# Expert weights of a two-layer encoder trunk: neighbouring contraction rows on one partition, 8 KB runs

## The chip, the cores and the metric

One core of a Trainium2 chip runs the whole program. The metric is the device time in microseconds (us). Weights stream from HBM through DMA engines into SBUF; TensorE (PE) multiplies, and leaves its products in PSUM, from where VectorE (DVE) and ScalarE (ACT) take them. SyncE (SP) issues nearly all weight transfers, GpSimd (POOL) helps with small work.

## The reference, cut to what matters

x is 256 tokens of 1024 features. Each of two layers has a mixer and then a mixture of experts (MoE), both behind an RMS norm that is modulated by a conditioning vector c, and everything is float32:

```
mod = silu(c) @ ada_w[layer] + ada_b[layer]          # six vectors of 1024
sh_m, sc_m, g_m, sh_f, sc_f, g_f = split(mod, 6)
h = rmsnorm(x, norm_mix_g[layer]) * (1 + sc_m) + sh_m
x = x + g_m * mixer(h)                               # layer 0 attention and RG-LRU, layer 1 S5 and GLU
h = rmsnorm(x, norm_ffn_g[layer]) * (1 + sc_f) + sh_f
# one group of 4 out of 4 groups, then 2 of its 4 experts for each token:
out = sum over experts e of gates[:, e] * ((silu(h @ w1[e]) * (h @ w3[e])) @ w2[e])
x = x + g_f * out
```

w1 and w3 of an expert are 1024 x 512, w2 is 512 x 1024: 2 MiB each, 96 such matrices in two layers, about 201 of the 285 MB that the program moves. A sum over the contraction index may be taken in any order, which is what the change uses.

## The kernel before, in words

**Stages.** Conditioning products and the mixer of layer 0, the MoE of layer 0, the S5 and GLU mixer of layer 1, the MoE of layer 1, the final norm. Engines are programmed apart and meet at semaphores; every order is written out by hand.

**The ring.** All big weights pass through `ring`, six slots of 16 KB per partition, one 2 MiB tile in each. SP walks through a fixed list (`ORDER`, 12 tiles for a group of 4 experts) and, for tile n, waits until the product on tile n-6 is done, then issues the transfer (`send_expert`, L355). `moe_src` (L322) takes the source from `w1_v`, `w3_v`, `w2_v` (L316 to L318).

**Layout.** In `(k p) f -> p k f` partition p of a w1 or w3 tile holds rows p, 128+p, 256+p and so on: eight separate rows of 512 floats, 2 KB each in HBM. For w2 they are four rows of 4 KB. Block k of the contraction is then features 128k to 128k+127.

**MoE of a layer** (`ffn(L)` on each engine). PE turns the normed x, computes router logits, and DVE makes one-hot `pick` matrices. Then a loop of four expert groups. In each, `gather_block` (L1687) multiplies 128 columns of `xhat` (the operand that is loaded) by `pick` (the one that streams), for 8 blocks k and 2 token halves, which gives the picked tokens with features on partitions; `hg_evac` (ACT L799 for even k, DVE L1267 for odd) scales and shifts each block by `modA[:, n, k]` and `mod[:, L, SH_F, k]` on the way out of PSUM. `product_up` (L1657) multiplies w1 and w3 tiles, `turn_he` (L1670) transposes the gated hidden rows in blocks of 128 columns (`tr`, L1402, whose loaded operand is the data), `product_down` (L1675) multiplies by w2, `scatter` (L1702) adds back to tokens. A group whose experts all have at most 64 tokens runs in a narrow form of half the streamed columns: seven of the eight groups here; the first group of layer 1 runs wide.

**Modulation columns.** Conditioning products land as rows; `ada_cols(i)` (L1437) turns batch i of them into columns by 4 matmuls with `sel`, DVE's `mod_evac(i)` (L961) adds the bias columns, `mod_scale` (L973) forms (1+scale) times the norm's gain. Biases and gains come by small transfers on ACT's queue at the start (L610 to L626), and PE turns them (L1476 to L1478).

Of the kernel before, what the change touches and what calls it, by code (L numbers as in the profile page):

```python
# [16 lines left out]
ALU = mybir.AluOpType  # L17
# [52 lines left out]
SH_M, SC_M, G_M, SH_F, SC_F, G_F = range(6)  # L70

# [33 lines left out]
def build(nc, a, out):  # L105
    ctx = ExitStack()
    with ctx:
# [26 lines left out]
        condc = sb("condc", [P, KD])  # L134
        wr_f = sb("wr_f", [P, 2 * KD * NR + 12])
# [31 lines left out]
        brow = yg[0:6 * KD, 1, 0:2 * P].rearrange("r (l p) -> r l p", l=2)  # L167

# [65 lines left out]
        warm = rt[:, 319:320]  # L234
        by_bge = lambda ap: ap.rearrange("p (b g e) -> p b g e", b=NB, g=NG)
# [80 lines left out]
        w1_v = a["moe_w1"].rearrange("l e (k p) f -> l p e k f", p=P)  # L316
        w3_v = a["moe_w3"].rearrange("l e (k p) f -> l p e k f", p=P)
        w2_v = a["moe_w2"].rearrange("l e (k p) n -> l p e k n", p=P)  # L318
# [10 lines left out]
        def _(sp_):  # L329
# [23 lines left out]
            def send_expert(L, j, group):  # L353
                w, e = ORDER[j]
                sp_.dma_start(u3(MOE_BASE[L] + j, D if w == "w2" else FF), moe_src(L, w, group * EPG + e)).then_inc(  # L355
                    S(f"loaded{(MOE_BASE[L] + j) % SLOTS}"), 16)
# [34 lines left out]
            for L in range(2):  # L391
# [19 lines left out]
                with sp_.If(n_over > 0):  # L411
                    with sp_.Fori(0, EPG // 2) as ee:
                        for j in range(SLOTS):
                            w = ("w1", "w3", "w2")[j % 3]

                            sp_.wait_ge(S(f"over_used{L}"), ee * SLOTS + (j + 1))
                            cw = D if w == "w2" else FF
                            sp_.dma_start(u3(j, cw), moe_src(L, w, grp * EPG + ee * 2 + j // 3)).then_inc(
                                S(f"over_in{L}_{j}"), 16)

                    sp_.wait_ge(S(f"over_used{L}"), SLOTS + 3 * EPG)
# [182 lines left out]
        def _(act):  # L604
# [20 lines left out]
            for L in range(2):  # L625
                act.dma_start(brow[:, L, :], a["ada_b"][L].rearrange("(r p) -> r p", p=P)).then_inc(S("rows_in"), 16)  # L626
            act.wait_ge(S("c_ps"), 1)
# [23 lines left out]
            def modulate(n):  # L651

                L, sec = n // 2, (SH_M if n % 2 == 0 else SH_F)
                act.wait_ge(S("modA_ready"), n + 1)
                for k in (0, 1, 4, 5):
                    act.wait_ge(S("xT_ps"), 4 * n + k // 2 + 1)
                    s.activation(hT[:, k, :], bank[k // 2][:, (k % 2) * T:(k % 2 + 1) * T], ACT.Identity, scale=modA[:, n, k:k + 1],
                                 bias=mod[:, L, sec, k:k + 1]).then_inc(S("hT_act"), 1)

            def gate_row(n):  # L660
# [13 lines left out]
                S("cols_ready"), 1)  # L674

# [106 lines left out]
            def ffn(L):  # L782
# [11 lines left out]
                if L == 0:  # L794
                    table_evac(0, 4)

                def hg_evac(k, at):

                    return s.activation(hg[k], bank[at], ACT.Identity, scale=modA[:, n, k:k + 1],  # L799
                                        bias=mod[:, L, SH_F, k:k + 1])  # L800
# [108 lines left out]
        def _(dve):  # L909
# [51 lines left out]
            def mod_evac(i):  # L961

                lo, hi = BATCHES[i]
                dve.wait_ge(S("ada_cols_ps"), i + 1)
                src = bank[6 if i == 0 else 7][:, 0:4 * (hi - lo)]
                units = lambda ap: ap.rearrange("p (u c) -> p u c", c=4)
                v.tensor_tensor(units(mod[:, :, :, :].rearrange("p l s k -> p (l s k)")[:, 4 * lo:4 * hi]),
                                src.rearrange("p (c u) -> p u c", c=4),
                                units(adab[:, :, :].rearrange("p l n -> p (l n)")[:, 4 * lo:4 * hi]),
                                ALU.add).then_inc(S("mod_cols"), 1)  # L970
                dve.wait_ge(S("mod_cols"), i + 1)

            def mod_scale(n):  # L973
# [4 lines left out]
                dve.wait_ge(S("modA_ready"), n + 1)  # L978
# [175 lines left out]
            mod_scale(2)  # L1154

# [21 lines left out]
            def ffn(L):  # L1177
# [87 lines left out]
                def hg_evac(k, at):  # L1265

                    return v.tensor_scalar(hg[k], bank[at], modA[:, n, k:k + 1], mod[:, L, SH_F, k:k + 1], ALU.mult, ALU.add)  # L1267
# [117 lines left out]
            mod_scale(3)  # L1385

# [11 lines left out]
        def _(pe):  # L1398
# [38 lines left out]
            def ada_cols(i):  # L1437
# [249 lines left out]
            def gather_block(k, narrow, at):  # L1687

                n_s = 64 if narrow else P
                for b in range(NB):  # L1690
                    last = mm(bank[at].rearrange("p (e n) -> p e n", n=P)[:, :, 0:n_s], xhat[:, b, k * P:(k + 1) * P],  # L1691
# [344 lines left out]
```

## Time and profile before

| | |
|---|---|
| median of 3 runs | 905.07 us (904.87 to 907.25) |
| span of the profiled execution | 902.3 us |
| PE busy | 828.3 us, 92% |
| DVE, ACT, POOL busy | 329.6, 199.7, 147.0 us |
| moved by DMA | 285.33 MB, mean 316 GB/s |

The page gives the profiled execution's span, from its first to its last instruction, and no other time of its own; 2.8 us lie between it and the median of the runs. PE is a busy share of overlapping, pipelined records and says little about who waits in a given stretch. The page's row of GB/s, 40 slices of 22.6 us, shows two long plateaus: the two MoE stages.

### The profile page before, as it was taken

To read this page: it belongs to the slowest core of one execution; us is meant where nothing else is said; L and a number is where in the kernel's file an instruction comes from. 1 tells how busy PE (TensorE), PEld (TensorE's weight loads), DVE (VectorE), ACT (ScalarE), POOL (GpSimd) and SP (SyncE) were. 2 spreads that over 40 slices of the span, in tenths; PEclk is the share of its full clock that TensorE was granted. 3 is DMA by queue.
4 is the path that set the end of the run, shared out by engine and by line. 5 is a ranking of instruction groups with operands and counts; after the bars stand their busy time and mean duration, and the time that the engine had idled before them with its cause. 6 is when DMAs were issued, how large, how long until landed. Compare 5 with 4: busy or idle time off the path is not lost.

```text
span 902.3 us, 12803 instructions
## 1 busy us (share of the span) xinstructions
PE 828.3 (92%) x5243; PEld 452.2 (50%) x5244; DVE 329.6 (37%) x718; ACT 199.7 (22%) x329; POOL 147.0 (16%) x234
## 2 busy tenths in 40 slices
PE   3899989889999999999599999689999899999994
PEld 1377644554465564643456543434444554655641
DVE  1447994681141221410799410621000311312304
ACT  2402331521221311311500110411001212213112
POOL 2328678194000000000033100000000000000000
PEclk9999999999999999999899999889999999999997
DMA  9999999978999999997996882206867299999992
GB/s 327 330 379 383 359 392 264 380 265 331 389 397 398 390 394 397 392 392 276 400 381 227 315 324 94 94 1 224 317 236 252 98 392 395 392 398 392 395 399 91
DMA packets 126290, 285.33 MB, mean 316 GB/s; under 512 B 7093, under 2 KB 8389, under 8 KB 125993
## 3 DMA queue, kind: packets, MB, share of 16 engines
q1 hardware_dynamic: 123552, 277.88, 83.9%
q0 software_dynamic: 1984, 5.21, 1.9%
q10 hardware_dynamic: 712, 1.67, 0.5%
q8 instruction: 29, 0.48, 0.2%
q14 instruction: 13, 0.10, 0.0%
HBM read 279.50 MB, written 5.24 MB: 316 GB/s over the span
## 4 chain that ended last, share of the span: by engine, by line
PE 75%; DMA 10%; DVE 6%; SPq 6%; issue 1%; ACT 1%; DVEq 0%; ACTq 0%
PE PS L1664 17%; PE PS L1683 12%; PE PS L1691 8%; PE PS L1707 6%; PE PS L1970 6%; PE PS L1667 6%; DMA ring<-in_moe_w 4%; SPq L355 4%; DMA ring<-in_ada_w 4%; PE PS L1433 3%; PE PS L1505 3%; PE PS L1403 3%; DMA ring<-in_ab_w_in 2%; PE PS L1488 2%; SPq L364 2%; PE PS L1622 2%
## 5 line engine op out<-in xcount | busy, mean ns | idle before, releaser
L1683 PE MATMUL PS<-ring,work 128*64 128x512 f32 (+1 forms) x512 | 128.8, 595 | 0.5 <-DMA ring<-in_moe_w 0.5
L1664 PE MATMUL PS<-ring,hT 128*64 128x256 f32 x896 | 109.6, 387 | 4.9 <-DMA ring<-in_moe_w 4.9
L1664 PE MATMUL PS<-ring,yg 128*64 128x256 f32 x896 | 106.4, 379 | 0.0
L1278 DVE TENSOR_TENSOR work<-work,PS 128x512 f32<-128x512 f32 x32 | 22.0, 688 | 201.2 <-PE PS L1664 152.9
L1664 PEld LDWEIGHTS PS<-ring,hT 128*64 128x64 f32 x896 | 62.9, 139 | 47.9 <-issue 11.8
L1664 PEld LDWEIGHTS PS<-ring,yg 128*64 128x64 f32 x896 | 64.5, 137 | 32.7 <-issue 0.5
L1683 PEld LDWEIGHTS PS<-ring,work 128*64 128x64 f32 (+1 forms) x512 | 42.8, 143 | 75.4 <-issue 71.1
L1282 DVE COPY yg<-PS 128x512 f32<-128x512 f32 x32 | 22.1, 692 | 145.7 <-PE PS L1683 145.7
L1691 PE MATMUL PS<-work,xhat 128*128 128x256 f32 (+1 forms) x256 | 68.4, 427 | 7.5 <-issue 7.1
L1707 PE MATMUL PS<-yg,grow 64*128 64x512 f32 (+1 forms) x256 | 68.0, 606 | 0.0
L1691 PEld LDWEIGHTS PS<-work,xhat 128*128 128x128 f32 x256 | 50.1, 198 | 28.5 <-issue 21.9
L1970 PE MATMUL PS<-ring,yg 128*128 128x512 f32 x128 | 58.7, 603 | 0.0
L818 ACT ACTIVATE yg<-PS 128x512 f32<-128x512 f32 x32 | 19.1, 598 | 157.6 <-PE PS L1683 157.6
L598 POOL TENSOR_TENSOR work<-work 128x512 f32<-128x512 f32 x7 | 9.0, 1279 | 272.8 <-DVE work L1368 256.7
L1433 PE MATMUL PS<-ring,condz 128*32 128x512 f32 x320 | 40.4, 627 | 12.7 <-DMA ring<-in_ada_w 12.7
L809 ACT ACTIVATE work<-PS 128x512 f32<-128x512 f32 x32 | 19.1, 598 | 105.9 <-PE PS L1664 80.6
L1707 PEld LDWEIGHTS PS<-yg,grow 64*128 64x128 f32 (+1 forms) x256 | 25.8, 187 | 31.2 <-issue 31.2
L1970 PEld LDWEIGHTS PS<-ring,yg 128*128 128x128 f32 x128 | 23.2, 190 | 33.6 <-issue 33.6
L813 ACT ACTIVATE work<-PS 128x512 f32<-128x512 f32 x32 | 19.1, 596 | 80.7 <-PE PS L1403 80.7
L1403 PE MATMUL PS<-ident,work 128*128 128x128 f32 x176 | 29.7, 291 | 6.3 <-DVE work L1278 3.1
L1267 DVE TENSOR_SCALAR hT<-PS,modA,mod 128x512 f32<-128x512 f32 x16 | 13.0, 810 | 56.9 <-PE PS L1691 56.9
L1403 PEld LDWEIGHTS PS<-ident,work 128*128 128x128 f32 x176 | 19.7, 144 | 25.5 <-issue 21.5
(366 smaller groups left out, 995.5 us busy)
## 6 DMA issues: line engine op xcount, KB each, us to landing
ring<-in_moe_w SPq DMA_DIRECT2D x96, 2048.0 KB, 17.8
ring<-in_ada_w SPq DMA_DIRECT2D x20, 2048.0 KB, 15.5
work<-in_ada_w SPq DMA_DIRECT2D x4, 2048.0 KB, 14.6
ring<-in_s_glu_w SPq DMA_DIRECT2D x4, 2048.0 KB, 17.0
ring<-in_ab_w_in SPq DMA_DIRECT2D x3, 2048.0 KB, 25.3
ring<-in_ab_w_out SPq DMA_DIRECT2D x2, 2048.0 KB, 14.7
ring<-rot_tables SPq DMA_DIRECT2D x2, 2048.0 KB, 11.1
rot_tables<-grow POOLq DMA_DIRECT2D x8, 256.0 KB, 5.7
```

What stands on the lines that cost most here:

```text
L355: sp_.dma_start(u3(MOE_BASE[L] + j, D if w == "w2" else FF), moe_src(L, w, group * EPG + e)).then_inc(S(f"loaded{(MOE_BASE[L] + j) % SLOTS ...
L1278: v.tensor_tensor(he[:, e % 2, :], he[:, e % 2, :], bank[1], ALU.mult).then_inc(S("he_ready"), 1)
L1282: v.tensor_copy(yg[:, e % 2, HALF:], bank[1 if e == 3 else 3]).then_inc(S("y_dve"), 1)
L1403: return nc.tensor.transpose(dst, src, ident[0:n, 0:n])
L1433: last = mm(bank[7][32 * j:32 * j + 32, :], condz[:, k, 32 - r:64 - r], ada_unit(u)[:, k, :], start=any(first) and k < 4, stop=any(final) ...
L1505: last = mm(dst, w[:, k, :], hT[:, k, :], start=k == 0, stop=k == KD - 1)
L1664: last = mm(dst[64 * u:64 * u + 64, 0:256], hg[k][:, e * P:e * P + 64], w[:, k, 256 * u:256 * u + 256], start=k == 0, stop=k == KD - 1)
L1667: last = mm(dst, hg[k][:, e * P:(e + 1) * P], w[:, k, :], start=k == 0, stop=k == KD - 1)
L1683: last = mm(dst, left[:, at:at + (64 if narrow else P)], w[:, c4, h * HALF:(h + 1) * HALF], start=c4 == 0, stop=c4 == KF - 1)
L1691: last = mm(bank[at].rearrange("p (e n) -> p e n", n=P)[:, :, 0:n_s], xhat[:, b, k * P:(k + 1) * P], pick[:, b, :, 0:n_s], start=b == 0, s ...
L1707: last = mm(acc[2 * b + h], pickT[pp, e, b * P:(b + 1) * P], yg[pp, at, h * HALF:(h + 1) * HALF], start=False, stop=False)
L1970: last = mm(bank[GLU_BANK[m][part]], actT[:, k, b * P:(b + 1) * P], u3(n)[:, k, :], start=False, stop=k == KD - 1)
```

## The change

The expert matrices are cut so that neighbouring contraction rows share a partition. Of w1 and w3, partition p holds rows 4p to 4p+3 of each half of 512 rows: two runs of 8 KB. Of w2 it holds rows 2p and 2p+1 of each half of 256: also two runs of 8 KB. Block k of the contraction is now features 512*(k//4) + 4*m + k%4 for m of 0 to 127. What goes into the products follows: `gather_block` loads every fourth column of `xhat`, `turn_he` every second column of `he`, and the experts get their own modulation columns `mod4` in the new order, from four more small transfers at the start, four small transposes and three copies, four more matmuls in `ada_cols(1)` and in `ada_cols(2)` that load every fourth column of the conditioning rows, one more addition in `mod_evac(1)` and `mod_evac(2)` and one `mod_experts` for each layer. Products, slots, their order and all byte counts of the weights stay.

```
-        w1_v = a["moe_w1"].rearrange("l e (k p) f -> l p e k f", p=P)
-        w3_v = a["moe_w3"].rearrange("l e (k p) f -> l p e k f", p=P)
-        w2_v = a["moe_w2"].rearrange("l e (k p) n -> l p e k n", p=P)
+        w1_v = a["moe_w1"].rearrange("l e (h p c) f -> l p e h (c f)", h=2, c=4)
+        w3_v = a["moe_w3"].rearrange("l e (h p c) f -> l p e h (c f)", h=2, c=4)
+        w2_v = a["moe_w2"].rearrange("l e (u p c) n -> l p e u (c n)", u=2, c=2)
...
-                sp_.dma_start(u3(MOE_BASE[L] + j, D if w == "w2" else FF), moe_src(L, w, group * EPG + e)).then_inc(
+                sp_.dma_start(u3(MOE_BASE[L] + j, SLOT // 2), moe_src(L, w, group * EPG + e)).then_inc(
...
+                act.dma_start(row4[4 * L:4 * L + 4, :], a["ada_b"][L, SH_F * D:G_F * D].rearrange(
+                    "(r n) -> r n", n=HALF)).then_inc(S("rows_in"), 16)
+                act.dma_start(row4[8 + 2 * L:10 + 2 * L, :], a["norm_ffn_g"][L].rearrange("(r n) -> r n", n=HALF)).then_inc(
+                    S("rows_in"), 16)
...
+            row4_t = bank[5][:, P:P + 48].rearrange("p (c n) -> p c n", c=4)
+            s.activation(by_c(mod4[:, :, :, :].rearrange("p l s k -> p (l s k)")), row4_t[:, :, 0:8], ACT.Copy)
+            for L in range(2):
+                last = s.activation(by_c(gain4[L]), row4_t[:, :, 8 + 2 * L:10 + 2 * L], ACT.Copy)
...
+                if i:
+                    dve.wait_ge(S("cols_ready"), 2)
+                    m4 = by_c(mod4[:, i - 1, :, :].rearrange("p s k -> p (s k)"))
+                    v.tensor_tensor(m4, bank[7][:, P:P + 16].rearrange("p (c m) -> p c m", c=4), m4, ALU.add)
...
+            def mod_experts(L):
+
+                v.scalar_tensor_tensor(mod4[:, L, 1, :], mod4[:, L, 1, :], 1.0, gain4[L], ALU.add, ALU.mult).then_inc(
+                    S("modA_ready"), 1)
+                dve.wait_ge(S("modA_ready"), MODX_AT[L])
...
-                    return v.tensor_scalar(hg[k], bank[at], modA[:, n, k:k + 1], mod[:, L, SH_F, k:k + 1], ALU.mult, ALU.add)
+                    return v.tensor_scalar(hg[k], bank[at], mod4[:, L, 1, k:k + 1], mod4[:, L, 0, k:k + 1], ALU.mult, ALU.add)
...
+                if i:
+                    f = r + 2
+                    for c in range(4):
+                        last = mm(bank[7][:, P + 4 * c:P + 4 * c + 4], arows[i][:, c::4], sel[:, f:f + 4], start=True,
+                                  stop=True)
...
-            pe.wait_ge(S("rows_in"), 16 * (len(ROWS) + 2))
+            pe.wait_ge(S("rows_in"), 16 * (len(ROWS) + 6))
             tr(bank[4][:, 0:N_ROWS], rows, N_ROWS)
+            for c in range(4):
+                tr(bank[5][:, P + 12 * c:P + 12 * c + 12], row4[:, c::4], 12)
...
-                    last = tr(bank[dst][:, c4 * P:(c4 + 1) * P], src[:, c4 * P:(c4 + 1) * P])
+                    f = c4 // 2 * 2 * P
+                    last = tr(bank[dst][:, c4 * P:(c4 + 1) * P], src[:, f + c4 % 2:f + 2 * P:2])
...
-                    last = mm(bank[at].rearrange("p (e n) -> p e n", n=P)[:, :, 0:n_s], xhat[:, b, k * P:(k + 1) * P],
+                    last = mm(bank[at].rearrange("p (e n) -> p e n", n=P)[:, :, 0:n_s], xhat[:, b, f + k % 4:f + HALF:4],
```

On PE the list of instructions differs in three places by added rows. The one between the tiles of the layer-0 output projection (L1622, `mix_out`) stood before like this; L1443 is `ada_cols(1)`, L1468 `gate_row`:

```order
L1433 MATMUL PS<-ring,condz 32x512 x24
L1622 MATMUL PS<-ring,yg 128x512 x4
L1443 MATMUL PS<-sel,work 128x12 x4
L1622 MATMUL PS<-ring,yg 128x512 x4
L1468 MATMUL PS<-ident,mod 128x128 x8
L1622 MATMUL PS<-ring,yg 128x512 x8
```

and stands now like this (line numbers of the changed kernel):

```order
L1656 MATMUL PS<-ring,yg 128x512 x4
L1470 MATMUL PS<-sel,work 128x12 x4
L1475 MATMUL PS<-sel,work 128x4 x4
L1656 MATMUL PS<-ring,yg 128x512 x4
L1500 MATMUL PS<-ident,mod 128x128 x8
L1656 MATMUL PS<-ring,yg 128x512 x8
```

Four matmuls of 4 streamed columns are new; the same four stand in `ada_cols(2)` among the GLU products. On DVE the same moment, `mod_evac(1)` with its scalings before the first residual rows (L1174 `tmp`, L1160 `add_rows`), was

```order
L1151 TENSOR_TENSOR yg<-hT,work 128x1024
L967 TENSOR_TENSOR mod<-PS,adab 128x48
L976 SCALAR_TENSOR_TENSOR modA<-mod,cols 128x8 x2
L1174 TENSOR_TENSOR xhat<-PS,grow 128x512
L1160 TENSOR_TENSOR x<-x,xhat 128x512
```

and is now

```order
L1176 TENSOR_TENSOR yg<-hT,work 128x1024
L983 TENSOR_TENSOR mod<-PS,mod 128x4x4
L986 TENSOR_TENSOR mod<-PS,adab 128x48
L995 SCALAR_TENSOR_TENSOR modA<-mod,cols 128x8 x2
L1001 SCALAR_TENSOR_TENSOR mod<-mod,work 128x8
L1200 TENSOR_TENSOR xhat<-PS,grow 128x512
L1186 TENSOR_TENSOR x<-x,xhat 128x512
```

Two small operations are added and nothing changes its place.

## Rows read from the trace of the kernel before

**Rows 1.** The page: span, and GB/s in 40 slices.

```profile
span 902.3 us, 12803 instructions
...
GB/s 327 330 379 383 359 392 264 380 265 331 389 397 398 390 394 397 392 392 276 400 381 227 315 324 94 94 1 224 317 236 252 98 392 395 392 398 392 395 399 91
```

**Rows 2.** Windows, one expert group each: us, busy times (instructions), PEclk, DMA share, GB/s.

```profile
246.66:305.93 59.27, 59.26 (x403) 33.04 (x401) 13.59 (x31) 13.35 (x19) 0.00 (x0) 1.00 1.04 395
365.19:428.56 63.37, 60.14 (x403) 32.68 (x401) 13.60 (x31) 13.54 (x20) 0.00 (x0) 1.00 0.93 351
767.80:827.03 59.23, 59.22 (x402) 33.01 (x400) 13.59 (x31) 13.34 (x19) 0.00 (x0) 1.00 1.04 395
827.03:889.14 62.11, 59.92 (x402) 32.84 (x400) 13.59 (x31) 13.54 (x20) 0.00 (x0) 1.00 0.92 350
```

**Rows 3.** Chain of waits, last group of layer 0: start us, us, what.

```profile
365.26 7.10 PE PS L1691 x32
...
400.22 21.08 DMA ring<-in_moe_w
...
421.34 3.65 PE PS L1683 x16
```

**Rows 4.** Timeline of PE, same group: start, us, instructions, [idle before <-releaser].

```profile
405.76 1.95 PE L1664 MATMUL PS<-ring,hT 128*64 128x256 f32 x16 [1.00 <-DMA ring<-in_moe_w]
...
411.18 1.95 PE L1664 MATMUL PS<-ring,hT 128*64 128x256 f32 x16 [1.74 <-DMA ring<-in_moe_w]
```

**Rows 5.** Windows by DMA rate: long stream, 2 KB, mostly 4 KB, 16 KB packets.

```profile
211.00:420.00 209.00, 206.00 (x1392) 112.64 (x1390) 43.66 (x98) 44.21 (x64) 2.02 (x2) 1.00 1.04 391
257.50:262.50 5.00, 5.00 (x48) 3.30 (x44) 2.72 (x10) 1.06 (x2) 0.00 (x0) 1.00 1.05 386
279.50:288.50 9.00, 9.00 (x58) 4.04 (x56) 1.38 (x2) 1.20 (x2) 0.00 (x0) 1.00 1.03 405
430.00:436.00 6.00, 3.10 (x112) 2.54 (x102) 5.66 (x11) 5.54 (x13) 0.00 (x0) 1.00 1.01 421
```

**Rows 6.** Instructions of L1691 and L1933: duration ns min/median/max, first and last start.

```profile
L1691 PEld LDWEIGHTS PS<-work,xhat x256: 186/190/337, 178.3 to 833.6; 128*128 128x128 f32 x128
L1691 PE MATMUL PS<-work,xhat x256: 379/379/1190, 178.3 to 833.8; 128*128 128x256 f32 x112, 128*128 128x512 f32 x16
...
L1933 PE MATMUL PS<-hT,work x256: 268/270/578, 440.9 to 491.5; 32*128 32x128 f32 x128
```

**Rows 7.** Groups with their shapes: busy us, mean ns.

```profile
L1664 PEld LDWEIGHTS PS<-ring,yg 128*64 128x64 f32 x896 | 64.5, 137 | 32.7 <-issue 0.5
...
L1403 PE MATMUL PS<-ident,work 128*128 128x128 f32 x176 | 29.7, 291 | 6.3 <-DVE work L1278 3.1 <-DVE work L1257 2.8 <-ACT work L778 0.4
...
L1505 PEld LDWEIGHTS PS<-hT,ring 128*128 128x128 f32 x128 | 23.9, 190 | 4.9 <-issue 1.7
...
L1955 PE MATMUL PS<-work 128*32 128x128 f32 x128 | 6.5, 276 | 0.0
```

**Rows 8.** Chain of waits, 141 to 166 us: start us, us, what.

```profile
143.54 3.63 PE PS L1622 x8
147.18 0.79 PE PS L1443 x8
147.97 3.53 PE PS L1622 x8
```

**Rows 9.** Timeline of DVE, 148 to 155 us.

```profile
154.50 0.69 DVE L1174 TENSOR_TENSOR xhat<-PS,grow 128x512 f32<-128x512 f32 x1 [5.88 <-ACT grow L667]
```

**Rows 10.** Timeline of PE, 10 to 26 us.

```profile
13.15 3.64 PE L1433 MATMUL PS<-ring,condz 128*32 128x512 f32 x16 [8.73 <-DMA ring<-in_ada_w]
...
23.75 1.92 PE L1433 MATMUL PS<-ring,condz 128*32 128x512 f32 x16 [1.28 <-DMA ring<-in_ada_w]
```

**Rows 11.** Timeline of ACT and its queue, 5.8 to 9 us.

```profile
5.86 0.83 ACTq L626 DMA_DIRECT2D yg<-in_ada_b  x2
...
8.23 0.21 ACT L630 ACTIVATE condz<-condc 128x8 f32<-128x8 f32 x1
```

More of the change, by code:

```diff
@@ L70 @@
 SH_M, SC_M, G_M, SH_F, SC_F, G_F = range(6)
+MODA_AT = (1, 2, 3, 5)
+MODX_AT = (4, 6)
 PRIMED = dict.fromkeys(('he_ready', 'y_dve', 'heT_ready', 'y_act', 'sil_ready'), 1)
@@ L134, in build @@
         condc = sb("condc", [P, KD])
+        mod4 = sb("mod4", [P, 2, 2, KD])
         wr_f = sb("wr_f", [P, 2 * KD * NR + 12])
@@ L167, in build @@
         brow = yg[0:6 * KD, 1, 0:2 * P].rearrange("r (l p) -> r l p", l=2)
+        row4 = yg[0:12, 0, HALF:D]
         o = W0
@@ L234, in build @@
         warm = rt[:, 319:320]
+        gain4 = (w3(WORK - 8, KD), rt[:, 308:316])
+        by_c = lambda ap: ap.rearrange("p (m c) -> p c m", c=4)
         by_bge = lambda ap: ap.rearrange("p (b g e) -> p b g e", b=NB, g=NG)
@@ L416, in _ @@
                             sp_.wait_ge(S(f"over_used{L}"), ee * SLOTS + (j + 1))
-                            cw = D if w == "w2" else FF
-                            sp_.dma_start(u3(j, cw), moe_src(L, w, grp * EPG + ee * 2 + j // 3)).then_inc(
+                            sp_.dma_start(u3(j, SLOT // 2), moe_src(L, w, grp * EPG + ee * 2 + j // 3)).then_inc(
                                 S(f"over_in{L}_{j}"), 16)
@@ L653, in modulate @@
                 L, sec = n // 2, (SH_M if n % 2 == 0 else SH_F)
-                act.wait_ge(S("modA_ready"), n + 1)
+                act.wait_ge(S("modA_ready"), MODA_AT[n])
                 for k in (0, 1, 4, 5):
@@ L674, in _ @@
                 S("cols_ready"), 1)
+            row4_t = bank[5][:, P:P + 48].rearrange("p (c n) -> p c n", c=4)
+            s.activation(by_c(mod4[:, :, :, :].rearrange("p l s k -> p (l s k)")), row4_t[:, :, 0:8], ACT.Copy)
+            for L in range(2):
+                last = s.activation(by_c(gain4[L]), row4_t[:, :, 8 + 2 * L:10 + 2 * L], ACT.Copy)
+            last.then_inc(S("cols_ready"), 1)
             def rows_out(i):
@@ L795, in ffn @@
                     table_evac(0, 4)
+                act.wait_ge(S("modA_ready"), MODX_AT[L])
                 def hg_evac(k, at):
-                    return s.activation(hg[k], bank[at], ACT.Identity, scale=modA[:, n, k:k + 1],
-                                        bias=mod[:, L, SH_F, k:k + 1])
+                    return s.activation(hg[k], bank[at], ACT.Identity, scale=mod4[:, L, 1, k:k + 1],
+                                        bias=mod4[:, L, 0, k:k + 1])
                 pt = lambda m: pickT[:, 2 * m:2 * m + 2, :].rearrange("p e t -> p (e t)")
@@ L977, in mod_scale @@
                                        ALU.add, ALU.mult).then_inc(S("modA_ready"), 1)
-                dve.wait_ge(S("modA_ready"), n + 1)
+                dve.wait_ge(S("modA_ready"), MODA_AT[n])
+            def mod_experts(L):
+                v.scalar_tensor_tensor(mod4[:, L, 1, :], mod4[:, L, 1, :], 1.0, gain4[L], ALU.add, ALU.mult).then_inc(
+                    S("modA_ready"), 1)
+                dve.wait_ge(S("modA_ready"), MODX_AT[L])
             def modulate(n):
@@ L1154, in _ @@
             mod_scale(2)
+            mod_experts(0)
             def add_rows(r, b, h, tmp):
@@ L1385, in _ @@
             mod_scale(3)
+            mod_experts(1)
             for m, (h, b) in enumerate(GLU_PAIRS):
@@ L1689, in gather_block @@
                 n_s = 64 if narrow else P
+                f = k // 4 * HALF
                 for b in range(NB):
-                    last = mm(bank[at].rearrange("p (e n) -> p e n", n=P)[:, :, 0:n_s], xhat[:, b, k * P:(k + 1) * P],
+                    last = mm(bank[at].rearrange("p (e n) -> p e n", n=P)[:, :, 0:n_s], xhat[:, b, f + k % 4:f + HALF:4],
                               pick[:, b, :, 0:n_s], start=b == 0, stop=b == NB - 1)
```

## The prediction

> **What bounds the kernel now.** I read the page first: the span is 902.3 us, and its GB/s row has two long plateaus of 390 to 399, the two MoE stages [rows 1]. A plateau means that the DMA engines may be the limit there, while PE also looks full. The windows, one per expert group, tell which. A narrow group in the middle of a layer takes 59.27 or 59.23 us, and PE is busy for all of it: PE is the limit. The last narrow group takes 63.37 us in layer 0 and 62.11 us in layer 1 for the same instructions, with PE busy for only 60.14 and 59.92 us [rows 2]. The chain of waits says what the last group waits for: it leaves PE, runs over a transfer issued at 400.22 us that lands 21.08 us later, and PE goes on at 421.34 [rows 3]. The timeline shows other pauses of 1.00 and 1.74 us with the same releaser [rows 4]. So DMA is a little slower than PE through a whole layer; six ring slots hide it until they are used up, and the bill comes in the last group: 63.37 - 59.26 = 4.11 us and 62.11 - 59.26 = 2.85 us, 6.96 us in all. That is all the whole stream costs, and all that a faster stream can give.
>
> How much slower it is: from 211 to 420 us the stream runs without a break at 391 GB/s [rows 5]. 209 us x 391 GB/s = 81.7 MB = 39 tiles of 2.097 MB, 5.36 us for a tile, 64.3 us for a group of 12, against PE's 59.26.
>
> **The packets.** A w1 or w3 tile now travels in packets of 2 KB, w2 in packets of 4 KB; afterwards both in 8 KB. The trace has no packet of 8 KB in this stream, but it has both sides: 386 GB/s in a stretch of 2 KB packets, 405 in one of mostly 4 KB, and 421 in the stretch where the rotation tables come in 16 KB runs [rows 5]. For one of 16 engines that is 16 x 2048 B / 386 = 84.9 ns and 16 x 4096 B / 405 = 161.8 ns. A line through the two is 8 ns for each packet and 76.9 ns for each 2 KB, so 8 KB take 315.6 ns: 415 GB/s, 5.05 us for a tile. Bounds: 5.43 us (2 KB rate, no gain) and 4.98 us (the 16 KB stretch). I take 5.05, between its neighbours. What is needed is less: without pauses the last w2 product of layer 0 would start at about 417.2 us (421.34 [rows 3] less 4.11), and 39 tiles from 211 us on must be in by then, 5.29 us each. At 5.05 they are in at 408, 9 us early. All 6.96 us go, and a better rate would give no more: PE's 59.26 us is next, and nothing else is late. **Term: -7.0 us.**
>
> The Trainium skill, page "DMA: Bandwidth & Descriptors", section "Specifications", gives 512 B as the smallest transfer for line rate; by it 2 KB packets already run at full rate and the sum would lose its first term. Rows 5 disagree with it by 5% between 2 and 4 KB.
>
> **The gather.** Every `gather_block` now loads every fourth float of xhat, one element in each 16 bytes: 2 records for each matmul, 32 for a group, 7 narrow groups, 224 records, and 32 in the wide one. No operand that PE loads is strided in the kernel before. The narrow gather takes 7.10 us for 32 records, 222 ns each [rows 3], and it is the streaming of 256 columns that sets this: L1691 streams in 379 ns records and loads in 190 [rows 6]. What a load itself occupies is seen where almost nothing is streamed: `ada_cols(1)`, 8 records in 0.79 us, 99 ns each [rows 8]. The slope agrees: 190 ns for 128 columns, 137 for 64 [rows 7], 0.83 ns a column, 106 for 128. So a load has 222 - 99 = 123 ns of cover in the narrow gather, about 320 in the wide one, which streams twice the columns. Ends for the price: none, if the load keeps its pace (and 0 is the floor; nothing here can make it quicker); three times the load, 297 ns, uncovers 75 ns x 224 = 17 us. The nearest row of a strided read by PE is L1933, which streams every second column of hT: its median is 270 ns against 276 for L1955, which streams 128 contiguous ones [rows 6, 7]. No price for 8 bytes of step. A doubled load (198 ns) still lies under 222, with some friction. I take 1 us in all, nearest to the row without a penalty.
>
> **The turns.** `turn_he` loads every second column: 2 transposes an expert in narrow groups, 4 in the wide one, 56 + 16 = 72. Each pays its load openly (the loop has no long stream beside it; a transpose record is 291 ns long, overlapped [rows 7]). At 8 bytes of step I take zero, by L1933. Upper end: a load doubled, +0.1 us x 72 = 7 us.
>
> **The modulation columns.** `ada_cols(1)` stands in the chain between two tiles of the output projection, PE without a pause [rows 8]; `ada_cols(2)` stands the same way among the GLU products. Each gains 4 matmuls, 8 records, that are all load: 8 x 99 ns = 0.8 us, or 1.6 us if fourfold steps double the load. Both are on the path: **+1.6 us** (end: +3.2). DVE's added work there, two operations of about 0.2 us, lies in the 5.88 us that it then waits for ACT [rows 9]; PE wants `mod_cols` only after 3.53 us more of products [rows 8]. The second `mod_evac` has the like cover, 2.7 us of GLU products before PE's `gate_row(2)`. `hg_evac` reads other columns of the same size: nothing.
>
> **The start.** Four more issues on ACT's queue, 0.83 us for two [rows 11], put the conditioning vector (8.23 us) back by 1.7 us; PE waits for weights until 13.15 [rows 10], cover 3 us. The four turns of 12 rows, about 0.5 us, lie before a pause of 1.28 us for the next tile at 23.75 [rows 10]; without that pause they would cost their 0.5 us. The three ACT copies come in the same long wait for weights. SP has fewer descriptors to push and never waits longer for it. Nothing.
>
> **Sum.** -7.0 + 1.0 + 0 + 1.6 = -4.4 us: a span of 897.9. Median over span was 905.07 - 902.3 = 2.8 us; the same around the new one gives **900.7 us**.
>
> **Rivals.**
>
> *Loads of one float in 16 bytes take double, the 8-byte ones don't.* For: such an operand is nowhere in the trace. Against: nothing but that. Gather 222 against 198: 1.5 us; columns 3.2 us. -7.0 + 4.7 = -2.3: 902.8 us. The Trainium skill, page "SBUF — State Buffer", section "Door 1", says that SBUF has 16-byte lines, wants two hits in each for full speed, and penalises each access to a new line. By this rule the gather and the columns pay and the turns, with two hits a line, don't. L1933, two hits a line, agrees; no row has one hit.
>
> *All strided loads double*, the turns too: -7.0 + 4.7 + 7.3 = +5: 910 us. L1933 speaks against.
>
> *The gather becomes load-bound.* A load of three times its pace, 297 ns, passes the 222 ns of streaming; from 2.2 times on it shows, and from about 245 ns a record (5 us / 224) it has eaten the gain. At three times: gather +17, columns 8 x 2 x 0.3 = 4.8, less 7.0: +15, 920 us; PE would then be so slow that even the old stream would keep up with it. For: load has one port and no spare in the trace for scattered reads. Against: the neighbour L1933.
>
> *The stream is no faster.* -0 + 2.6: 907.7 us. It would take no more than 391 GB/s at 8 KB; 405 and 421 speak against it [rows 5].
>
> **How the numbers follow.** Forecast 0.60, first rival 0.16, all double 0.07, load-bound gather 0.08, stream no faster 0.06, 0.03 for what I don't see. A measurement of this kernel tells about 0.3% from no change, 2.7 us: faster is under 902.35, slower over 907.8. Forecast nearly all faster (0.57), first rival a third (0.05): faster 0.62. Same: the rest of these two and most of the stream's case, 0.20. Slower: 0.18. Range: from 898.0 (no cost at all: 905.07 - 7.0) to 908.0, which takes in the stream's case and leaves out the two last slower ones.
>
> **What would show it.** The last groups at 59.3 + the gather's price instead of 63.37 and 62.11, no PE pause with the releaser moe_w; the plateaus near 395 to 415 with pauses in the stream, PE being slower; a middle group's length minus 59.26 is the price of gather and turns; the gather's loads at 190 ns if the pace holds, 290 if doubled; 1.6 us in place of 0.79 for the columns. Wrong if middle groups grow by over 1 us, or if the last groups still wait for moe_w.

## The result and the profile after

The changed kernel takes 911.09 us (median of 8 runs, 906.97 to 912.09), the kernel before 905.2 us in the runs beside it: a ratio of 1.005, with a 95% interval of 1.003 to 1.0071, so 2.7 to 6.4 us slower (the ratio is not the quotient of the two medians, which lie 5.9 us apart). I had forecast 900.7 us, 898.0 to 908.0, and gave slower a chance of 0.18. The forecast was wrong in its sign. The execution that was profiled is the fastest of the 8 (906.97 us, span 905.2), so its span says less than its parts. Medians here and below leave out four executions that were slow as a whole, over 1000 us: one of the kernel before, one of the layout alone, two of the first run with the columns moved.

The page of the changed kernel, to be read beside [rows 1]: span, GB/s in 40 slices, the stream's queue, and the median time from issue to landing of a weight tile.

```profile
span 905.2 us, 12855 instructions
...
GB/s 325 330 378 382 359 394 295 397 203 330 422 359 423 422 412 423 412 425 143 395 347 231 324 303 59 148 2 191 294 258 256 117 405 421 414 424 422 415 280 71
...
q1 hardware_dynamic: 66208, 277.88, 79.0%
...
ring<-in_moe_w SPq DMA_DIRECT2D x96, 2048.0 KB, 12.0
```

The packets of that queue fell from 123552 to 66208 and the landing from 17.8 us to 12.0, and the plateaus of 390 to 399 now stand mostly at 412 to 425 (405 to 424 in layer 1): the stream did become quicker, by somewhat more than my 415 GB/s in most slices. What PE makes of it is in the windows of the changed kernel, one narrow group each (a middle and the last one of layer 0, the same two of layer 1), which answer to [rows 2]:

```profile
248.64:308.76 60.12, 60.12 (x402) 35.03 (x400) 13.58 (x31) 13.34 (x19) 0.00 (x0) 1.00 0.96 399
368.89:429.02 60.13, 60.13 (x403) 35.03 (x401) 13.59 (x31) 13.54 (x20) 0.00 (x0) 1.00 0.76 313
771.83:831.96 60.13, 60.13 (x403) 35.04 (x401) 13.58 (x31) 13.33 (x19) 0.00 (x0) 1.00 1.01 419
831.96:892.09 60.13, 60.13 (x403) 35.04 (x401) 13.59 (x31) 13.54 (x20) 0.00 (x0) 1.00 0.74 306
```

Two things are to be seen. The last groups are no longer longer than the middle ones and PE is busy from end to end: the 6.96 us of waiting for weights are gone. And every group, the middle ones too, is 0.87 us longer than the 59.26 us of before. The weight loads (PEld, the second busy time) rose from 33.04 to 35.03 us. The chain of waits of the last group of layer 0, beside [rows 3]:

```profile
368.96 7.77 PE PS L1727 x32
...
402.80 0.44 PE PS L1430 x2
403.23 1.92 PE PS L1743 x8
405.15 3.58 PE PS L1718 x16
...
418.00 0.44 PE PS L1430 x2
418.43 7.02 PE PS L1718 x32
425.45 3.63 PE PS L1743 x16
```

No DMA stands in it any more. The gather (L1727) takes 7.77 us for 32 records instead of 7.10, so 243 ns each instead of 222, the start of the block included. Two turns (L1430) take 0.44 us. The instructions of the gather and of the strided column products (L1475), beside [rows 6]:

```profile
L1727 PEld LDWEIGHTS PS<-work,xhat x256: 307/329/332, 180.6 to 839.2; 128*128 128x128 f32 x128
L1727 PE MATMUL PS<-work,xhat x256: 397/397/1210, 180.6 to 839.4; 128*128 128x256 f32 x112, 128*128 128x512 f32 x16
```

```profile
L1475 PEld LDWEIGHTS PS<-sel,work x8: 309/329/329, 148.3 to 149.9; 128*128 128x128 f32 x8
L1475 PE MATMUL PS<-sel,work x8: 370/374/374, 148.3 to 149.9; 128*128 128x4 f32 x8
L1475 PEld LDWEIGHTS PS<-sel,yg x8: 310/329/329, 521.2 to 522.8; 128*128 128x128 f32 x8
```

A load of every fourth float has a record of 329 ns; it was 190. Last, the chain of the changed kernel around its columns, in the output projection (beside [rows 8]) and in the GLU stage:

```profile
147.63 0.80 PE PS L1470 x8
148.43 1.86 PE PS L1475 x8
150.28 3.54 PE PS L1656 x8
```

```profile
520.54 0.79 PE PS L1470 x8
521.33 1.86 PE PS L1475 x8
523.19 4.38 PE PS L2006 x6
527.56 1.78 PE PS L1500 x16
```

Eight records with a 16-byte step take 1.86 us, 232 ns each. The eight contiguous ones before them take 0.79 us on this chain, but that isn't eight times a load. The trace of the kernel before has the loads of its first such place (L1443) by themselves:

```profile
146.59 0.19 PEld L1443 LDWEIGHTS PS<-sel,work 128*128 128x128 f32 x1 [0.24 <-issue]
147.01 0.86 PEld L1443 LDWEIGHTS PS<-sel,work 128*128 128x128 f32 x7 [0.24 <-issue]
```

The first load starts 0.42 us before the others, under the last product of the output projection tile, and the other seven follow each other at (0.86 - 0.19) / 6 = 112 ns. So a contiguous load takes 112 ns, not the 99 ns of the prediction, and the 16-byte step makes it 2.1 times as long. And behind the second set the six GLU products take 4.38 us. In a window of the trace over just these:

```profile
523.19:527.57 4.38, 4.38 (x8) 1.84 (x9) 1.30 (x5) 0.60 (x1) 0.00 (x0) 0.61 1.02 426
```

PEclk, the number behind the busy times, is 0.61: most of that stretch ran at 1.2 GHz instead of 2.4.

### The profile page after: what moved, and what is told of

Same layout as the page of the kernel before. It is cut to its first block, busy times and chain, and to the rows that moved or that the text cites. A ratio compares the mean times of both kernels' runs of the same rounds, so it can differ in the third digit from the quotient of the medians.

```text
span 905.2 us, 12855 instructions
## 1 busy us (share of the span) xinstructions
PE 840.3 (93%) x5263; PEld 474.8 (52%) x5264; DVE 330.4 (37%) x722; ACT 200.1 (22%) x332; POOL 146.8 (16%) x234
## 3 DMA queue, kind: packets, MB, share of 16 engines
q1 hardware_dynamic: 66208, 277.88, 79.0%
## 4 chain that ended last, share of the span: by engine, by line
PE 83%; DVE 10%; DMA 3%; SPq 2%; issue 1%; ACT 1%; DVEq 0%; ACTq 0%
PE PS L1698 21%; PE PS L1718 14%; PE PS L1727 8%; PE PS L1743 7%; PE PS L2006 7%; PE PS L1701 6%; PE PS L1430 3%; PE PS L1656 3%; PE PS L1460 3%; DMA ring<-in_ab_w_in 2%; PE PS L1522 2%; PE PS L1991 2%; PE PS L1539 2%; SPq L370 2%; DVE work L1283 1%
## 5 line engine op out<-in xcount | busy, mean ns | idle before, releaser
L1727 PE MATMUL PS<-work,xhat 128*128 128x256 f32 (+1 forms) x256 | 71.0, 436 | 7.2 <-issue 6.8
L1727 PEld LDWEIGHTS PS<-work,xhat 128*128 128x128 f32 x256 | 62.7, 326 | 19.0 <-issue 16.0
L1460 PE MATMUL PS<-ring,condz 128*32 128x512 f32 x320 | 43.1, 666 | 10.3 <-DMA ring<-in_ada_w 10.3
L1430 PE MATMUL PS<-ident,work 128*128 128x128 f32 x176 | 31.7, 303 | 6.5 <-DVE work L1283 3.2
L1430 PEld LDWEIGHTS PS<-ident,work 128*128 128x128 f32 x176 | 23.6, 171 | 25.6 <-issue 21.1
L1293 DVE TENSOR_SCALAR hT<-PS,mod 128x512 f32<-128x512 f32 x16 | 13.0, 810 | 57.2 <-PE PS L1727 57.2
```

Source lines behind the costliest of these rows:

```text
L1430: return nc.tensor.transpose(dst, src, ident[0:n, 0:n])
L1460: last = mm(bank[7][32 * j:32 * j + 32, :], condz[:, k, 32 - r:64 - r], ada_unit(u)[:, k, :], start=any(first) and k < 4, stop=any(final) ...
```

## The experiments

The theory after this profile: the layout gives what I forecast, and three things that PE does pay more than it, namely the gather's load at a 16-byte step, the turns' load at 8 bytes, and the columns, these with a stretch of slow clock behind them. The rival: something about the new stream itself (longer packets, other times of arrival) slows PE, and the layout is to blame. Runs of one set share their runs of the kernel before, whose medians were 905.54, 904.84 and 904.58 us in the three sets. In the kernels that have the layout, the gather or the turns alone, or the gather or the columns' step put back, the gathered features, the experts' columns and the weight rows no longer belong to each other, so their output is wrong; the products and their shapes are the same, and so are the eight expert groups, seven narrow and one wide.

**The changed kernel once more.**

> The changed kernel once more, timed and with a second profile. Theory: its time is set by work on PE that both profiles show (gather 7.77 us a group in place of 7.10, modulation columns +1.86 us at each of two places), so the second profile has the same lengths and a span near 909, with the rest in windows of the 1.2 GHz level. Rival: something that varies from run to run (a pause, a transfer) adds some 4 us, and the second profile shows it at one place.

910.67 us, ratio 1.0059 (1.0039 to 1.0079). Groups of 60.12, columns 1.86, GLU stage 75.22 us: the lengths repeat. What does vary between executions, whatever the kernel, is how many short stretches PE spends at 1.2 GHz: the first 3.9 us of the output projection (121.53 to 125.41 us) have a granted clock of 0.61 in the changed kernel's profile, and the same stretch (121.68 to 125.35 us) 1.00 in that of the kernel before; the mean over the span lies between 0.966 and 0.977 in the fourteen profiles. This moves a time by some us, so a term of 1 us is read from the trace below, not from medians.

**The layout alone.** Kernel before, with the three views and the tile shape of the change, nothing else:

```diff
-        w1_v = a["moe_w1"].rearrange("l e (k p) f -> l p e k f", p=P)
+        w1_v = a["moe_w1"].rearrange("l e (h p c) f -> l p e h (c f)", h=2, c=4)
...
-        w2_v = a["moe_w2"].rearrange("l e (k p) n -> l p e k n", p=P)
+        w2_v = a["moe_w2"].rearrange("l e (u p c) n -> l p e u (c n)", u=2, c=2)
```

> The kernel before with only the weights' layout and packets changed (features and weight rows don't match then; gather, turns and columns load contiguously as before). Theory: the stream's pauses were worth 7.0 us, so 898 us, last groups at 59.3 us. Rival: the faster stream costs something elsewhere, and the time is 902 us or more.

899.56 us, ratio 0.9938 (0.9913 to 0.9963): 3.4 to 7.9 us faster. Windows of its third and its last group of layer 0:

```profile
309.18:368.44 59.26, 59.25 (x403) 33.03 (x401) 13.58 (x31) 13.33 (x19) 0.00 (x0) 1.00 1.01 422
368.44:427.70 59.26, 59.26 (x403) 33.03 (x401) 13.59 (x31) 13.53 (x20) 0.00 (x0) 1.00 0.79 323
```

This settles the rival: the new stream at 422 GB/s runs beside groups of exactly the old 59.26 us. The last group is as short as a middle one, so the term of -7.0 us holds, and no part of a group's growth comes from the stream.

**The gather alone.** Kernel before, with

```diff
+                f = k // 4 * HALF
...
-                    last = mm(bank[at].rearrange("p (e n) -> p e n", n=P)[:, :, 0:n_s], xhat[:, b, k * P:(k + 1) * P],
+                    last = mm(bank[at].rearrange("p (e n) -> p e n", n=P)[:, :, 0:n_s], xhat[:, b, f + k % 4:f + HALF:4],
```

> The kernel before with only the gather's loaded operand taken from every fourth column (it then gathers other features than the weights and scales expect). Theory: each narrow gather takes 7.77 us in place of 7.10, but the old stream sets the end of both layers, and 4 x 0.67 in layer 0 and 3 x 0.67 in layer 1 are less than its pauses of 4.1 and 2.9 us: within 1 us of before. Rival: the gather is on the path, +4.7 us.

905.74 us, ratio 1.0015 (0.9995 to 1.0035), about 1.4 us. By the total my low price looks right. The windows of a middle and the last group of layer 0 say otherwise:

```profile
247.62:307.48 59.86, 59.86 (x403) 34.60 (x401) 13.59 (x31) 13.35 (x19) 0.00 (x0) 1.00 1.04 391
367.33:429.25 61.92, 60.30 (x402) 34.43 (x400) 13.59 (x31) 13.54 (x20) 0.00 (x0) 1.00 0.94 355
```

The middle group grew by 0.60 us. The last one shrank from 63.37 to 61.92 although it does the same extra work: with the slow stream, a slower PE only waits less at the end. The price is there, and in this kernel it is mostly paid out of the pauses. The total of this run answers another question than the one I had asked.

**The columns alone.** Kernel before, with the four added products in `ada_cols`, whose results nobody reads:

```diff
+                if i:
+                    f = r + 2
+                    for c in range(4):
+                        last = mm(bank[7][:, P + 4 * c:P + 4 * c + 4], arows[i][:, c::4], sel[:, f:f + 4], start=True,
+                                  stop=True)
```

> The kernel before with only the four strided matmuls added in ada_cols(1) and ada_cols(2) (nobody reads their result). Theory: +1.86 us at each, 3.7 us, and up to 1.7 us more where PE's clock falls behind the second: 909 to 911 us. Rival: they hide behind the wait for ACT or DVE: under +1 us.

909.74 us, ratio 1.0061 (1.0036 to 1.0085): sixteen records (eight at each place) cost 3.3 to 7.7 us, 5.5 by the ratio, where I had taken 1.6. The trace splits it: 1.86 us of records at each of two places, and behind the second ones

```profile
522.47 1.86 PE PS L1448 x8
524.33 4.30 PE PS L1975 x6
```

4.30 us for six products at a granted clock of 0.64. These take 2.68 us in the layout alone.

**The turns alone.** Kernel before, with

```diff
-                    last = tr(bank[dst][:, c4 * P:(c4 + 1) * P], src[:, c4 * P:(c4 + 1) * P])
+                    f = c4 // 2 * 2 * P
+                    last = tr(bank[dst][:, c4 * P:(c4 + 1) * P], src[:, f + c4 % 2:f + 2 * P:2])
```

> The kernel before with the turns' sources at a step of 8 bytes alone (the weights' layout as before, so the expert output is wrong in the order of its contraction rows). Theory (+66 ns a strided record, partly on the path): narrow middle group 59.26 to 59.5, seven groups 1.4 us where no pause covers it: 906.0 to 906.6. Rival (an 8-byte step is free): every group as before, within 0.5 us of the kernel before.

906.28 us, ratio 1.0015 (0.9993 to 1.0037); the total can't tell the two theories apart. The trace can, with the same two groups of layer 0:

```profile
249.17:308.71 59.54, 59.53 (x403) 33.54 (x401) 13.59 (x31) 13.34 (x19) 0.00 (x0) 1.00 1.04 394
368.24:430.58 62.34, 60.19 (x403) 33.24 (x401) 13.59 (x31) 13.54 (x20) 0.00 (x0) 1.00 0.94 353
```

A middle group grows by 0.27 us, 8 turns of 34 ns. Their records, four turns of a narrow group in the kernel before and then in this one:

```profile
L1403 PEld LDWEIGHTS PS<-ident,work x4: 139/140/141, 292.6 to 295.0; 128*128 128x128 f32 x4
```

```profile
L1403 PEld LDWEIGHTS PS<-ident,work x4: 194/206/223, 295.3 to 297.7; 128*128 128x128 f32 x4
```

**Only w2 and the turns put back.** The changed kernel with `w2_v` and `turn_he` as before.

> The changed kernel with w2's layout and the turns as before (w1 and w3 in 8 KB runs, gather and columns at 16 bytes). Theory (the turns' 8-byte step is paid, some 66 ns a record on 72 records of a group): narrow groups fall from 60.13 to 59.9, seven of them 1.5 us: 909.5. Rival (it is free, the group's growth is all the gather's): groups stay at 60.1, time 911.

907.73 us, ratio 1.003 (1.0012 to 1.0047). Groups are 59.86 us long, as the theory said. The time is below both of the recorded figures. Against the changed kernel's ratios of 1.005 and 1.0059 it is 1.8 to 2.6 us less, which the turns' 1.9 us account for. This profiled execution has no slow stretch in the GLU stage (73.52 us against 75.21). Its chain at that place:

```profile
523.22 1.86 PE PS L1475 x8
525.08 2.68 PE PS L2005 x6
```

So the slow stretch follows these columns often, not always.

**Only the gather put back.** The changed kernel with contiguous loads in `gather_block`.

> The changed kernel with the gather's loads contiguous, all else kept (its hidden rows are then in the wrong order for the weights, so the expert output is wrong). Theory (the gather's load at 16 bytes is the bound of the block): narrow groups fall from 60.13 to 59.53 (the turns' 0.27 stays), seven groups 4.2 us: 906.5 to 907. Rival (the groups' growth comes from the stream of 8 KB packets): groups stay above 59.9, 910 or above.

905.37 us, ratio 1.0008 (0.9986 to 1.003). By the ratios that is 3.8 to 4.6 us under the changed kernel, about the 4.2 us of the theory, though the median lies below the 906.5 to 907 of the expectation. Groups are 59.53 us. Note the contrast with the gather alone: the same edit is worth about 4 us here and about 1.4 us there, the second with an interval of -0.5 to +3.2. PE is the limit in the one and shares it with DMA in the other.

**Only the columns' step put back.** The changed kernel with as many column products, their loads contiguous:

```diff
-                        last = mm(bank[7][:, P + 4 * c:P + 4 * c + 4], arows[i][:, c::4], sel[:, f:f + 4], start=True,
+                        last = mm(bank[7][:, P + 4 * c:P + 4 * c + 4], arows[i][:, c * P:(c + 1) * P], sel[:, f:f + 4], start=True,
```

> The changed kernel with the four added column products of each ada_cols call loading neighbouring floats instead of every fourth (as many products, in the same place; the experts' shift and scale are then taken from the wrong columns, so the expert output is wrong). Theory (the stride makes each of the 16 loads 233 ns instead of 112, and the slow window follows them): 16 x 121 ns = 1.9 us and 1.7 to 3.4 us of slow clock less: 911 - 3.6 to 5.3 = 906 to 907.5. Rival (it is the added products as such, strided or not): 909 or above.

909.43 us, ratio 1.0031 (1.001 to 1.0053). The expectation failed: the median is not in the 906 to 907.5 of the theory but in the range of its rival, 909 or above. By the ratios it is 1.7 to 2.5 us under the changed kernel, where the step alone should give 1.9. The total doesn't decide between the two; the chain of its GLU stage shows that both have a part:

```profile
525.37 0.89 PE PS L1475 x8
526.26 2.68 PE PS L2006 x6
```

The added records as such take 0.89 us, their step the rest of the 1.86, and no slow stretch follows: the stage is 72.55 us. The profiled execution still spans 909.3 us, with a mean clock of 0.966, the lowest of all the profiles; its first group alone takes 69.68 us against 67.99. How much of the missing 2 us is such scatter isn't settled by the medians; the intervals overlap.

The lengths of all these fit one sum. Narrow groups, middle and last of layer 0, us, from windows between the groups' first gather records:

| kernel | gather step | turns step | middle | last |
|---|---|---|---|---|
| before | - | - | 59.27 | 63.37 |
| layout alone | - | - | 59.26 | 59.26 |
| turns alone | - | 8 B | 59.54 | 62.34 |
| gather alone | 16 B | - | 59.86 | 61.92 |
| w2 and turns back | 16 B | - | 59.86 | 59.86 |
| gather back | - | 8 B | 59.53 | 59.53 |
| changed | 16 B | 8 B | 60.12 | 60.13 |

59.26 + 0.60 + 0.27 = 60.13. The GLU stage from the last S5 product to the last GLU product is 71.64 us before; 72.55 with eight added records whose loads are contiguous (+0.90); 73.52 with the 16-byte step (+0.97); 75.13 to 75.22 with the slow stretch (+1.70), in four of the five profiled executions with that step at this place, and in none of the nine others.

**A version with shorter steps.** The theory says what to do: the stream only needs to beat 5.29 us a tile, for which 4 KB packets might do, and those need a step of 8 bytes only. w1 and w3 in pairs of rows; w2, whose runs are 4 KB already, and the turns as before, the columns following in pairs too; against the changed kernel:

```diff
-        w1_v = a["moe_w1"].rearrange("l e (h p c) f -> l p e h (c f)", h=2, c=4)
+        w1_v = a["moe_w1"].rearrange("l e (h p c) f -> l p e h (c f)", h=4, c=2)
...
-        w2_v = a["moe_w2"].rearrange("l e (u p c) n -> l p e u (c n)", u=2, c=2)
+        w2_v = a["moe_w2"].rearrange("l e (k p) n -> l p e k n", p=P)
...
-                f = k // 4 * HALF
+                f = k // 2 * 2 * P
...
-                    last = mm(bank[at].rearrange("p (e n) -> p e n", n=P)[:, :, 0:n_s], xhat[:, b, f + k % 4:f + HALF:4],
+                    last = mm(bank[at].rearrange("p (e n) -> p e n", n=P)[:, :, 0:n_s], xhat[:, b, f + k % 2:f + 2 * P:2],
```

> The changed kernel with w1 and w3 in runs of 4 KB (two neighbouring rows to a partition) and w2 as before: the gather and the strided columns read every second float (8 bytes), the turns are contiguous again. Theory (a strided load costs what its step makes it: 232 to 243 ns a record at 16 bytes, some 165 ns at 8 bytes, read from the turns' mean that rose 144 to 171 ns over 176 records of which 72 are strided): the gather's loads fit under the 222 ns of its products, so a narrow group is back at 59.3 us; the stream's 6.9 us stay won; the columns cost 2 x 8 x 66 ns = 1.1 us over before, and the window at half clock in the GLU stage costs 1.7 us if it still follows: 905.2 - 7.0 + 1.1 + 1.7 = 901 (899 to 902). Rival (a step of 8 bytes costs the gather as much as one of 16): narrow groups stay at 59.9, and the time is 905 or above.

899.22 us, ratio 0.9939 (0.9915 to 0.9963): it beats both kernels, the changed one by 10 to 11 us by the ratios. Its page's GB/s row, its two groups, the gather's and the columns' records:

```profile
GB/s 329 327 378 385 357 393 288 390 224 338 410 386 410 410 410 410 409 410 240 395 339 223 319 330 88 99 3 195 309 247 265 106 377 410 410 410 410 409 374 72
```

```profile
246.97:306.24 59.27, 59.26 (x403) 33.23 (x401) 13.59 (x31) 13.33 (x19) 0.00 (x0) 1.00 1.01 401
365.50:424.77 59.27, 59.26 (x403) 33.24 (x401) 13.59 (x31) 13.53 (x20) 0.00 (x0) 1.00 0.87 345
```

```profile
L1726 PEld LDWEIGHTS PS<-work,xhat x256: 193/196/336, 180.3 to 833.5; 128*128 128x128 f32 x128
L1726 PE MATMUL PS<-work,xhat x256: 379/379/1190, 180.3 to 833.7; 128*128 128x256 f32 x112, 128*128 128x512 f32 x16
```

```profile
517.67 0.94 PE PS L1475 x8
518.61 2.68 PE PS L2005 x6
```

Every part is as the theory has it, or better: at an 8-byte step the gather's load is 196 ns against 190 and its products keep their 379 ns; eight column records take 0.94 us, 118 ns each; no slow stretch follows. A tile at 410 GB/s takes 5.11 us, so a group's 12 tiles need 61.4 us and the stream is still a little slower than PE's 59.27. But it is within the 5.29 us a tile that six ring slots forgive, and no pause is left. All of the gain of 8 KB is had from 4 KB.

**The same once more.**

> The kernel with w1 and w3 in 4 KB runs once more, beside the next: 899 (898 to 901), narrow groups 59.27.

901.21 us, ratio 0.995 (0.9927 to 0.9974), narrow groups of 59.27 again. The median is just over the expected 898 to 901; it is faster than before in both sets.

**And with the columns moved.** Of that version, the added column products stand where PE waits for x, and DVE's part of them goes behind `modulate` (the filler product `keep_busy` ahead of the router writes to another bank, which is not shown below):

```diff
+            expert_cols(0)
             pe.wait_ge(S("x_new"), 1)
...
+            pe.wait_ge(S("x_part"), 6)
+            expert_cols(1)
             pe.wait_ge(S("x_new"), 3)
```

> As half, and the four strided column products leave ada_cols and stand ahead of PE's waits for the new x before each ffn, where PE idles; VectorE's addition and the scale for the experts follow behind modulate. Theory: the columns' 1.1 us and the slow window behind them leave the path (GLU stage back at 71.7 us, mix stage at 37.8 to 40.1): 898.5 (897 to 900), at or below the layout alone at 900.1. Rival (VectorE's two more instructions behind modulate stand in the routing chain and cost as much, or the slow window comes wherever the strided loads are): 901 or above.

> The same with the column products moved, once more. Theory (the 1.0 us of the GLU stage is won, nothing lost; its 902.6 of the first time came from slow windows that come and go): within 1.5 us of half_again. Rival (the move costs something in every execution): 2.5 us or more above half_again, with one stage longer than in half.

901.31 us and ratio 0.9966 (0.9943 to 0.9989) the first time, 900.64 us and 0.9944 (0.992 to 0.9967) the second, beside 899.22 and 901.21 of the version without the move. The GLU stage in the second profile is 71.66 us against 72.60:

```profile
490.16:561.82 71.66, 71.66 (x412) 33.80 (x405) 20.26 (x41) 6.29 (x11) 5.02 (x4) 1.00 0.65 244
```

and the stretch from the first router product to the first gather is 13.12 us with and without the move, so DVE's two later instructions cost nothing. The 0.94 us is won in the trace. In the medians it can't be told from the scatter, one time for and one against; the first expectation (897 to 900) failed, with a median in its rival's range, and I don't claim the move as a gain.

## Why the prediction was wrong

**What bounds the kernel, and the stream: right.** The last groups fell to the length of the middle ones, no pause for the expert weights was left in the trace, and the layout alone gives 0.9938. Its size, 8 KB at 415 GB/s, was a little low: packets of 8 KB took 309 ns (median) where the line gave 315.6, and the plateaus reached 425. That a better rate would give no more was right too, and could have been taken further. "What is needed is less", 5.29 us a tile: the nearest row, 405 GB/s at 4 KB, is 5.18. I had the numbers to see that half of the change would do, and didn't ask.

**"`ada_cols(1)`, 8 records in 0.79 us, 99 ns each": the first step that failed.** It is a misreading of [rows 8]: the 0.79 us hold seven loads, the first having begun under the product before, and a load takes 112 ns. What I built on 99 went wrong with it: the doubled load and the columns' price came out too low, the cover too large. The slope in the same paragraph, 106 ns for 128 columns, was nearer.

**"A doubled load (198 ns) still lies under 222, with some friction. I take 1 us in all": failed with it.** The load with the 16-byte step takes 233 ns. That is close to a doubling of the true 112, which would be 224 and no longer under 222. Nor was 222 the pace inside the block, since it has the block's start in it. All 32 loads of the last group of layer 0, before and after:

```profile
365.19 6.77 PEld L1691 LDWEIGHTS PS<-work,xhat 128*128 128x128 f32 x32 [0.76 <-issue]
```

```profile
368.89 7.54 PEld L1727 LDWEIGHTS PS<-work,xhat 128*128 128x128 f32 x32 [0.76 <-issue]
```

With the last record (190 and 329 ns) taken off and 31 steps counted, they follow each other at 212 ns and at 233. The second is the 233 ns of the columns, where next to nothing is streamed beside the loads: the loads now set the block's time. Cost: 7 groups x 0.60 = 4.2 us. The mechanism is that of my third rival, the load-bound gather, which I priced at three times and gave 0.08; its bound "from 2.2 times on it shows" should have been 1.9 or 2.0. The only row that I set against it was of another kind: L1933 streams a strided operand, while the gather loads one. A row for the operand that is streamed said nothing here about the one that is loaded.

**"At 8 bytes of step I take zero, by L1933": failed for the same reason.** The price is 34 ns a turn, 7 x 0.27 = 1.9 us. It lay in the range I gave (0.1 us x 72). Of the wide group's 16 turns no run here gives a price: it is 117.8 us long before and 117.14 after, with slow stretches that lie elsewhere.

**"8 x 99 ns = 0.8 us": the added columns were mis-sized.** Each place costs 1.86 us, 3.7 in both: 16 x 112 for the records as such and 16 x 121 for their step. My upper end, 3.2, was still below.

**What was not in the sum at all:** the slow stretch behind the second columns, +1.7 us at that place in four of five profiles. Whether the whole kernel pays it is open. The first narrow group of layer 1, before and after:

```profile
706.86:767.77 60.91, 60.90 (x400) 34.14 (x400) 13.59 (x31) 13.35 (x19) 0.00 (x0) 0.97 0.80 300
```

```profile
711.73:771.83 60.10, 60.10 (x401) 35.01 (x401) 13.57 (x31) 13.33 (x19) 0.00 (x0) 1.00 0.80 328
```

Before, this group has a slow stretch of its own and is 1.7 us longer than a middle one; after, it has none. So it is in all profiles: the four with the stretch behind the columns have none here, and nine of the ten others have one, which costs 1.1 to 1.7 us. In the profiles the one nearly makes up for the other, and no run tells whether that is chance.

The sum with what was measured is -7.0 + 4.2 + 1.9 + 3.7 = +2.8 us, and +4.5 with the slow stretch, against a measured +2.7 to +6.4, and +3.5 to +7.1 the second time. The three prices on PE, 9.8 us together, turn the gain into a loss by themselves; the last 1 to 2 us are not settled. DVE's and ACT's added work and the four turns at the start show no cost of their own, as forecast, but 1 us wouldn't be seen: the first product of the output projection starts between 121.68 and 123.03 us in the five profiles without that work and between 121.53 and 124.94 in the nine with it.

**The rivals.** The 16-byte loads doubled and the 8-byte ones free, my second likeliest, had the right places for the gather and columns and, at 2.1, nearly the right factor. Its price for the gather, 1.5 us against 4.2 measured, was low because it doubled 99 ns. The page "SBUF — State Buffer" of the Trainium skill, section "Door 1", wants two hits in each 16-byte line for full speed. In the columns and the gather the runs agree: two hits a line cost 118 against 112 ns in the columns and nothing in the gather's pace, one hit costs 233 in both. In the turns they don't: two hits a line make the load 206 instead of 140 ns, and here the measurement decides. The rule pointed to the right sign for the two big terms, with no number; I gave it 0.16 on the strength of a row that did not bear on it. The range ended at 908.0 and the median was 911.09: it left out the load-bound gather, whose mild form is what happened.

## What to carry to other kernels

Before a layout change that is paid for with strided reads, ask which operand of the matmul becomes strided. Here streaming it was free (270 ns against 276) while loading it wasn't, and a load hides only as far as the products beside it are long. Bound that factor by the cover, and treat a cover near twice the load as no cover. Measure the load between the starts of loads in the middle of a row: where the first of them starts early, total time over count comes out too low (99 against 112 ns here). Ask also how much of the faster stream is needed, and take the smallest step that gives it: 4 KB runs and 8-byte steps gave the whole gain here, 8 KB runs and 16-byte steps lost it. And don't price a part by adding it alone to a kernel that another engine holds back: the gather cost 1.4 us there (-0.5 to +3.2) and about 4 us in the kernel whose stream had become quick.

## What the runs showed of the hardware

- Loading 128 columns of float32 takes 112 ns a record in a row of loads with contiguous columns, 118 with every second, 233 with every fourth. The records read 192, 196 and 329 ns, so a record's length is not its pace.
- The load of a transpose is another case: 140 ns contiguous, 206 with every second column. Why it suffers from a step of 8 bytes, and the load of a product hardly does, stays open.
- A stretch of about 4.3 us at a granted clock of 0.61 to 0.64 followed eight loads at 16-byte steps that had only four columns each to stream, in the midst of GLU products that ran at 2.4 GHz, in four of five profiled executions. At that place, eight contiguous ones, or eight at 8 bytes, were not followed by it in any profile, nor were the strided ones in the fifth. PE had streamed next to nothing for 2.65 us before it (0.79 and 1.86), for 1.73 us in the version with 4 KB runs; whether this or something else decides wasn't tried. In two executions (the second of the changed kernel and the one with w2 and the turns put back) a stretch at 1.2 GHz followed the first columns too.
- For one DMA engine, packets of 2, 4, 8 and 16 KB took 87, 162, 309 and 611 ns (medians on the stream's queue, the third in the changed kernel and the others in the kernel before); 16 x size over time is 377, 405, 424 and 429 GB/s. From 4 KB on there is little left to win. The Trainium skill, page "DMA: Bandwidth & Descriptors", section "Specifications", has line rate from 512 B on; these runs disagree by 12% between 2 and 8 KB.
